# Splitting each expert's 64 slots into 32 per tile of tokens in a two-layer mixer and mixture-of-experts kernel

## The reference, cut to what matters

```
for l in range(2):
    x = layer_norm(alpha * x + mixers(x @ w_in[l]) @ w_out[l])
    score = sigmoid(x @ router_w)                  # 256 x 16
    best group of 4 experts, best 2 experts in it  # per token
    gate = the 2 scores, divided by their sum
    for e in range(16):
        h = silu(x @ w_gate[l][e]) * (x @ w_up[l][e])     # 1024 -> 512, twice
        out += gate[:, e:e+1] * (h @ w_down[l][e])        # 512 -> 1024
    x = layer_norm(alpha * x + out)
```

## Time and profile before

| | |
|---|---|
| time, median of 3 runs | 875.36 us (875.27 to 876.86) |
| span of the profiled execution | 876.5 us, mean granted TensorE clock 0.975 |
| TensorE busy | 832.4 us (95%) |
| DVE, ACT, POOL busy | 320.5, 182.2, 25.9 us |
| moved by DMA | 245.83 MB |
| experts' part, layer 0 and layer 1 | about 204 to 430 and 637 to 863 us |

### The profile page before, as it was taken

The page is one execution under the profiler, slowest core; times in us unless marked ns, Lnnn a source line. Parts: engine busy times, 40 slices in busy tenths (PEclk is TensorE's granted clock), DMA queues, the critical chain, the costliest instruction groups (busy, mean ns, idle before and its releaser), DMA issues. The chain is left out here.

```text
span 876.5 us, 12763 instructions
## 1 busy us (share of the span) xinstructions
PE 832.4 (95%) x5339; PEld 459.3 (52%) x5339; DVE 320.5 (37%) x644; ACT 182.2 (21%) x371; POOL 25.9 (3%) x101
## 2 busy tenths in 40 slices
PE   9999999989999999999799998999799999999994
PEld 8888666456334333333388876754543343333331
DVE  1296446474112111111434955292732211111215
ACT  1142323233001120000313233241330011100001
POOL 7100000000000000000000000000000000000000
PEclk9999999989999999999889999999899999999997
DMA  8944200496999999999944522025959999899992
GB/s 277 314 163 167 97 3 15 160 424 223 352 422 421 422 391 368 422 420 422 396 145 150 192 98 98 2 97 209 402 201 362 423 422 421 337 424 421 421 421 94
DMA packets 55249, 245.83 MB, mean 280 GB/s; under 512 B 8356, under 2 KB 13328, under 8 KB 30608
## 3 DMA queue, kind: packets, MB, share of 16 engines
q1 hardware_dynamic: 53840, 240.20, 69.3%
q0 software_dynamic: 1344, 4.72, 1.6%
HBM read 243.85 MB, written 1.05 MB: 279 GB/s over the span
## 5 line engine op out<-in xcount | busy, mean ns | idle before, releaser
L1047 PE MATMUL bank<-x_cm,ring 128*128 128x256 f32 x576 | 127.7, 383 | 0.9 <-ACT x_cm L2015 0.9
L549 PE MATMUL bank<-ring,xg 128*64 128x512 f32 x544 | 123.6, 596 | 2.0 <-issue 2.0
L1047 PEld LDWEIGHTS bank<-x_cm,ring 128*128 128x128 f32 x576 | 110.3, 192 | 17.3 <-ACT x_cm L2015 1.2
L780 DVE TENSOR_TENSOR y_lo<-bank,y_hi 128x512 fp32r<-128x512 f32 x32 | 22.1, 692 | 200.1 <-issue 179.8
L549 PE MATMUL bank<-ring_more,xg 128*64 128x512 f32 x416 | 94.6, 596 | 0.2 <-DMA ring_more<-in_exp_w_up 0.2
L549 PEld LDWEIGHTS bank<-ring,xg 128*64 128x64 f32 x544 | 37.5, 137 | 71.1 <-issue 69.4
L583 PE MATMUL bank<-ring,x_cm 128*64 128x512 f32 x256 | 61.2, 623 | 1.0 <-DVE g_col L756 1.0
L583 PE MATMUL bank<-ring_more,x_cm 128*64 128x512 f32 x256 | 58.2, 596 | 2.0 <-issue 2.0
L765 DVE TENSOR_SCALAR x_cm<-bank,g_col 128x512 f32<-128x512 f32 x32 | 24.0, 751 | 94.4 <-PE bank L549 79.7
L1054 PE MATMUL bank<-ring,x_cm 128*128 128x512 f32 x128 | 57.7, 599 | 0.0
L549 PEld LDWEIGHTS bank<-ring_more,xg 128*64 128x64 f32 x416 | 29.8, 137 | 52.9 <-issue 51.5
(11 more groups left out here) (387 smaller groups left out, 928.3 us busy)
## 6 DMA issues: line engine op xcount, KB each, us to landing
ring<-in_exp_w_gate SPq DMA_DIRECT2D x36, 1024.0 KB, 12.3
ring<-in_exp_w_up SPq DMA_DIRECT2D x36, 1024.0 KB, 12.9
ring_more<-in_exp_w_down SPq DMA_DIRECT2D x32, 1024.0 KB, 12.9
ring<-in_exp_w_down SPq DMA_DIRECT2D x32, 1024.0 KB, 11.8
ring_more<-in_exp_w_gate SPq DMA_DIRECT2D x26, 1024.0 KB, 12.5
ring_more<-in_exp_w_up SPq DMA_DIRECT2D x26, 1024.0 KB, 14.7
ring<-in_w_in SPq DMA_DIRECT2D x24, 1024.0 KB, 8.1
ring<-in_w_out SPq DMA_DIRECT2D x8, 1024.0 KB, 6.2
```

What stands on the lines that cost most here:

```text
L549: m = T.matmul(b[half_of(n, i), :], xg[g][:, 4 * h + k, cols], w[:, k, :], start=(h == 0 and k == 0), stop=(h == 1 and k == 3))
L780: mark(V.tensor_tensor(y_lo[:], y_bank(n, N)[:], y_hi[:].bitcast(F32), ALU.subtract), "v_ylo")
L1047: m = T.matmul(out_, w[:, k, c:c + n], x_cm[:, k, :], start=(k == 0), stop=(k == KD - 1))
```

## The change

An expert's 64 slots are no longer shared by both tiles: 32 (`HS`) belong to tile 0 and 32 to tile 1, and the running numbers start anew in each tile, with 128 added in tile 1. A branch flag is raised when an expert has more than 32 tokens in one tile.

- `pick[:, j]` has 256 columns instead of 512, and a gather's products have 256 columns each and write their own half of the bank. ACT puts the columns in the order expert, tile, slot while it copies.
- The scatter is still 8 products, each with 32 rows instead of 64; the four products of one part of y lie in four different groups of 32 rows.
- `position_row` is four products of 32 output partitions by 128 columns instead of one of 128 by 256; `pick_t` is compared over 128 columns.
- `slot_gates` has 16 products with 32 weight columns each, writing 32 partitions, instead of 8 products with 128.
- The count of the slots takes two products instead of five, and the positions are made in two DVE instructions, each followed by its tile's `pick`.

```diff
-        pick = sb("pick", [P, TT, GU * SL], F32R)
+        pick = sb("pick", [P, TT, GU * HS], F32R)
-        pick_t = sb("pick_t", [P, S], F32R)
+        pick_t = sb("pick_t", [P, P], F32R)
-        CROWD = SL + 0.5
+        CROWD = HS + 0.5
...
-                    m = T.matmul(out_[:], x[:, j, k, :], pick[:, j, :],
-                                 start=(j == 0 and x is x_hi), stop=(j == TT - 1 and x is x_lo))
+                    m = T.matmul(out_[:, GU * HS * j:GU * HS * j + GU * HS], x[:, j, k, :], pick[:, j, :],
+                                 start=(x is x_hi), stop=(x is x_lo))
...
-                    for j in range(TT):
-                        w = gate[:, j, e:e + 2] if rounds == 1 else gate[:, j, e:e + 1].to_broadcast([P, 2])
-                        m = T.matmul(b_y[:, u:u + 2], pick[:, j, u * SL:u * SL + 2 * SL].bitcast(F32), w,
-                                     start=(j == 0), stop=(j == TT - 1))
+                    for i in range(2):
+                        for j in range(TT):
+                            w = gate[:, j, e:e + 2] if rounds == 1 else gate[:, j, e:e + 1].to_broadcast([P, 2])
+                            at_slot = SL * i + HS * j
+                            m = T.matmul(b_y[at_slot:at_slot + HS, u:u + 2],
+                                         pick[:, j, (u + i) * HS:(u + i) * HS + HS].bitcast(F32), w, start=True, stop=True)
...
-                            ps = slice(SL * hf, SL * hf + SL)
-                            m = T.matmul(bank[2 * j + hf][:], pick_t[ps, tile_(j)], y[ps, :], start=(n == 0 and y is y_hi),
+                            ps = slice(SL * hf + HS * j, SL * hf + HS * j + HS)
+                            m = T.matmul(bank[2 * j + hf][:], pick_t[ps, :], y[ps, :], start=(n == 0 and y is y_hi),
...
-                mark(T.matmul(b_hid[n % 2][:, 0:S], ident_b[0:NE, e:e + 1].to_broadcast([NE, P]), pos_t[:],
-                              start=True, stop=True), "t_prow")
+                for q in range(P // HS):
+                    m = T.matmul(b_hid[n % 2][HS * q:HS * q + HS, 0:P], ident_b[0:NE, e:e + 1].to_broadcast([NE, HS]),
+                                 pos_t[:, tile_(q % TT)], start=True, stop=True)
+                mark(m, "t_prow")
...
-            return A.activation(out_, in_, ACT.Identity, scale=ln_cm[:, l, 0, k:k + 1], bias=ln_cm[:, l, 1, k:k + 1])
+            return A.activation(out_.rearrange("p (u j s) -> p j u s", u=GU, j=TT),
+                                in_.rearrange("p (j u s) -> p j u s", u=GU, j=TT), ACT.Identity,
+                                scale=ln_cm[:, l, 0, k:k + 1], bias=ln_cm[:, l, 1, k:k + 1])
...
-                T.matmul(bank[5][:, 0:NE], tri_b[:], sel_b[:, 0], start=True, stop=True)
-                T.matmul(bank[5][:, NE:2 * NE], tri_b[:], sel_b[:, 1], start=True, stop=False)
-                T.matmul(bank[5][:, NE:2 * NE], ones_b[:], sel_b[:, 0], start=False, stop=True)
-                T.matmul(bank[5][:, 2 * NE:3 * NE], ones_b[:], sel_b[:, 0], start=True, stop=False)
-                inc(T.matmul(bank[5][:, 2 * NE:3 * NE], ones_b[:], sel_b[:, 1], start=False, stop=True), "t_slots")
+                chosen = sel_b[:].rearrange("p j e -> p (j e)")
+                T.matmul(bank[5][:, 0:TT * NE], tri_b[:], chosen, start=True, stop=True)
+                inc(T.matmul(bank[5][:, TT * NE:2 * TT * NE], ones_b[:], chosen, start=True, stop=True), "t_slots")
...
-                do(V.scalar_tensor_tensor(out=pos[:], in0=bank[5][:, 0:TT * NE].rearrange("p (j e) -> p j e", j=TT), scalar=1.0,
-                                          in1=rank, op0=ALU.add, op1=ALU.mult))
-                for j in range(TT):
+                for j in range(TT):
+                    do(V.scalar_tensor_tensor(out=pos[:, j], in0=bank[5][:, NE * j:NE * j + NE], scalar=1.0 + P * j,
+                                              in1=rank[:, j], op0=ALU.add, op1=ALU.mult))
                     inc(pick_slots(0, 1, (j,)), "v_first")
```

More of the change, by code:

```diff
@@ L54, in hybrid_trunk @@
     SL = 64
+    HS = SL // TT
     ROUNDS = S // SL
@@ L453, in pick_slots @@
                 m = V.tensor_tensor(pick[:, j, :].rearrange("p (e s) -> p e s", e=per),
-                                    slot_row[:, 0:SL * rounds].unsqueeze(1).to_broadcast([P, per, SL * rounds]),
-                                    pos[:, j, g * per:g * per + per].unsqueeze(2).to_broadcast([P, per, SL * rounds]),
+                                    slot_row[:, P * j:P * j + HS * rounds].unsqueeze(1).to_broadcast([P, per, HS * rounds]),
+                                    pos[:, j, g * per:g * per + per].unsqueeze(2).to_broadcast([P, per, HS * rounds]),
                                     ALU.is_equal)
@@ L787, in turned_pick @@
                     dve.wait_ge(*at("t_scat", n))
-                mark(V.tensor_scalar(pick_t[:], b_hid[n % 2][:, 0:S], slot_col[:, r:r + 1], None, ALU.is_equal), "v_pick_t")
+                mark(V.tensor_scalar(pick_t[:], b_hid[n % 2][:, 0:P], slot_col[:, r:r + 1], None, ALU.is_equal), "v_pick_t")
             picks(0)
@@ L951, in _ @@
             step(G.iota(slot_row[:], [[1, S]], base=1, channel_multiplier=0, allow_small_or_imprecise_dtypes=True))
-            for h in range(2):
-                step(G.iota(slot_col[SL * h:SL * h + SL, :], [[SL, ROUNDS]], base=1, channel_multiplier=1,
+            for q in range(P // HS):
+                step(G.iota(slot_col[HS * q:HS * q + HS, :], [[HS, ROUNDS]], base=1 + P * (q % TT), channel_multiplier=1,
                             allow_small_or_imprecise_dtypes=True))
@@ L1971, in _ @@
                 dve.wait_ge(*done("t_slots", l))
-                do(V.scalar_tensor_tensor(out=pos[:], in0=bank[5][:, 0:TT * NE].rearrange("p (j e) -> p j e", j=TT), scalar=1.0,
-                                          in1=rank, op0=ALU.add, op1=ALU.mult))
                 for j in range(TT):
+                    do(V.scalar_tensor_tensor(out=pos[:, j], in0=bank[5][:, NE * j:NE * j + NE], scalar=1.0 + P * j,
+                                              in1=rank[:, j], op0=ALU.add, op1=ALU.mult))
                     inc(pick_slots(0, 1, (j,)), "v_first")
-                do(V.tensor_reduce(rms_s[:, 0, 1:2], bank[5][:, 2 * NE:3 * NE], AX.X, ALU.max))
+                do(V.tensor_reduce(rms_s[:, 0, 1:2], bank[5][:, TT * NE:2 * TT * NE], AX.X, ALU.max))
                 inc(V.tensor_scalar(crowded[:], rms_s[:, 0, 1:2], CROWD, None, ALU.is_gt), "v_flag")
```

## The result

The changed kernel takes 864.1 us (median of 4 runs, 862.2 to 866.47) against 875.32 us for the kernel before (4 runs, 873.3 to 876.86): a ratio of 0.9876, with a 95% interval of 0.985 to 0.9903, or 9 to 13 us less. The forecast was 860.0 us in a range of 854.5 to 867.5, so the time lies in the range, on its slow side. The gain is 11 us where 15 were expected. The profiled execution is the 866.47 us one, with a span of 864.6 us; before it was 876.5, so the two profiles differ by 11.9 us, and what follows splits up this figure.

What follows compares the result with a forecast made beforehand. TensorE and the weight-load queue were taken to end together, the queue being late next. Its 6.8 us plus 0.8 behind `hidden(15, 1)` make 7.6 a layer, 15.2 in all: 861.3 on the profile, 860 against the median, range 854.5 to 867.5.

Steps and rivals of the forecast that it cites:

- a faster TensorE alone: Rival for the whole kernel: TensorE sets the end after all, 13.0 us a layer gained, 849 us; chance 0.03.
- second hole: Drop in load traffic mid-part, lacking 4.0 us in layer 0 and 4.4 in layer 1; forecast to close, counted 3.8.
- The release that closes the hole: `hidden(8, 0)` frees the slot for `gate8`: forecast 8.9 us earlier, where 7.0 (7.4 in layer 1) were needed.
- the start of a part: First experts of each layer: `first_half` starts 1.95 us earlier, `hidden(0, 1)` and the releases after it 3.0.
- first hole: Low load traffic at the start of the experts, lacking 9.0 us; loads there wait for TensorE's next step.
- The queue's gain: Weight loads of each layer: 3.0 us earlier from the start plus 3.8 from the middle, 6.8 in all.
- Gate products: `slot_gates`: 32 records at 0.068 us, 2.1 against 1.84 us, so a loss of 0.3 us per group.
- Half clock: Rival: 1.2 GHz spells ahead of `hidden(0, 1)` or behind `hidden(15, 1)`, 1.9 us each, 862 to 866 us; chance 0.13.
- Gathers: Gather products of 256 columns follow each other every 0.122 us; a gather of four saves 0.42 us.
- The rule of the Trainium skill that was kept as a rival: Rival, only the scatter gains: a gather product's load and stream don't overlap, 218 ns each, 867 us; chance 0.08.
- Scatter: Each expert's scatter: quads of 32-row products run side by side, 0.66 us instead of 1.13, saving 0.47.
- The tail: Behind `hidden(15, 1)` in each layer: two scatters and two position rows, 0.8 us saved.

Runs made afterwards that it cites:

- gather_twice: Changed kernel with every gather product issued twice, the first of each pair overwritten: 868.08 us, ratio 0.9893 to the kernel before.
- the second profile: Changed kernel measured again with no edit: 865.16 us, ratio 0.9874 to the kernel before; this profile's span is 862.2 us.
- The edit of one count: Changed kernel, but DVE gives a count right behind the gate values and the first group's gate products wait for that: 860.21 us, ratio 0.9807.
- turn_pad: Changed kernel with one overwritten 256-column product more ahead of the transposes of experts 0 to 13: 866.65 us, ratio 0.9892 to the kernel before.
- light_after: Changed kernel with half of the columns of all loads of experts 8 to 15 left out: 848.4 us, ratio 0.9691 to the kernel before.
- before: The kernel before the change, unedited: 875.32 us.
- light_before: The kernel before with half of the columns of all loads of experts 8 to 15 left out: 874.87 us, ratio 0.9977.
- order_before: The kernel before with down7 loaded ahead of gate8 and up8: 875.91 us, ratio 0.9995.

## Why the prediction was right, and where it was off

**The bound was read rightly.** TensorE and the queue ended together before; a faster TensorE alone would have given 849, and the measured 848.4 with light loads answers to that. The queue then set the end in layer 0, at a place and in a form that were forecast: waits for up weights in experts 12 to 15, the longest 2.43 us where 2.9 were computed, and a closed second hole in both layers. In layer 1 the same waits are there, but `hidden(15, 1)` itself came 0.6 us behind its weights. (That 422 GB/s is "never exceeded" is loosely said: slices in the earlier trace rows reach 424. It changes nothing.) The agreement of 848.4 with 849 is closer than it deserves, as the next points show: it is in part luck.

**The release that closes the hole came 9.1 us earlier in layer 0** (329.56 became 320.49), where 8.9 were computed, but the terms are others. Computed: 3.0 for the start, 3.3 for scatters, 3.4 for gathers, -0.8 for position rows and gate products. Measured: 0.75 at the start, 7 steps x 0.19 = 1.3, 8 gathers x 0.45 = 3.6, and 3.1 around expert 4's gate products, 8.8 in all. Errors of 2.3 us (the start) and 1.5 (scatters with position rows) on one side and of 3.4 (gate products) on the other cancelled; that is luck. With a start that is hardly earlier, 4.0 us would have been enough to close the hole, and `gather_twice` shows it: its release is 4.65 earlier (324.91), and no dip is left.

**The step that fell short: the start of a part, "`hidden(0, 1)` and the releases after it come 3.0 us earlier".** It named ACT's four copies as late next. In layer 0 it was DVE's queue, 2.54 us, and then the half clock, 1.6 us; the releases came 2.1 and 0.75 earlier, and the first hole did not shrink at all. In the second profile, without the spell, the later of the two releases came 3.4 earlier, so this part of the prediction holds in some executions and not in others. In layer 1, where DVE was late by only 0.29 us, the second of them is 4.0 earlier, more than the 3.0. The prediction had looked at what the gathers wait for and what reads them, but not at the wait ahead of the gate products (`v_pick`), whose count DVE gives behind work that nobody at this place needs. The edit of one count is worth 4 to 6 us, and with it the kernel is at the 860 that was forecast; since the edit was no part of the forecast and other terms were off too, that figure is a coincidence. The queue's gain, 6.8 us by the prediction, was 3.5 in layer 0 and 7.4 in layer 1: the 3.3 us that are missing in layer 0 are as much as the 15.2 of the forecast lack against the 11.9 of the profile.

**Gate products: "+0.3 per group" was mis-sized and had the wrong sign.** They cost 1.4 us less, and no half clock follows in expert 4, another 1.7. The price came from a row of products that stream 128 columns each; these stream two. With 128 weight columns such a record costs 115 ns, with 32 it costs 13. The Trainium skill has a rule on the load ("TensorE: Matmul & The Clock Gate", LDWEIGHTS (loading the stationary operand)): it takes as many nanoseconds as it has weight columns, divided by 1.2, whatever the rows. That is 107 ns for 128 columns, with which the 0.11 of the earlier trace rows agrees, and 27 ns for 32, an estimate by that page of 0.85 us for 32 records. The trace has 0.43, half of that: on the same side as the rule and further. Why it is half, no run shows.

**Half clock: it was a rival of 0.13 and in part it came true,** ahead of `hidden(0, 1)` as it said, in one of two profiles of the changed kernel. What it did not say is that the change also takes spells away: those in expert 4. Two more stand behind waits for weights, in both profiles: the one at 385.26 (2.43 us of wait) lies under the queue, as TensorE waits again at 400.16 and 410.11, and the one at 825.18 (2.42) takes some 0.6 us. That is less than the 1.9 of the rival, which had put its spells where nothing is left to hide them.

**Gathers: 0.12 us per product, as forecast,** 0.45 us per gather where 0.42 were. The rule of the Trainium skill that was kept as a rival ("TensorE: Matmul & The Clock Gate", Part 3, What overlaps and what doesn't), that a load overlaps running products only for other rows of the array, doesn't hold here: these products have all 128 rows, and their loads of 0.19 us start every 0.12 us, under each other and under the streams.

```profile
206.54 0.19 PEld L427 LDWEIGHTS bank<-pick,x_lo 128*128 128x128 f32 x1
206.66 0.19 PEld L427 LDWEIGHTS bank<-pick,x_hi 128*128 128x128 f32 x1
```

**Scatter: 0.67 us, forecast 0.66.** But its saving of 0.47 is not a step's saving. The step shrank from 12.47 to 12.28 us, 0.19: the turn needs DVE's scaling of the hidden values, which takes 0.75 us from the last hidden product on. Before, the scatter of 1.13 hid it; now TensorE waits 0.24. Position rows gave 0.05 instead of costing 0.06. "What is late next" was asked about the start of a part and not about the step. Here it costs next to nothing, since the queue sets the pace there (`turn_pad`). It would be up to 28 x 0.24 us if TensorE did, an estimate.

**The tail** gave 0.53 per layer up to the start of `scatter(15)`: 0.48 for `scatter(14)`, 0.05 for a position row. The 0.47 of `scatter(15)` itself isn't seen in what follows in layer 0, since the next layer's first products are 4.06 us earlier (431.55 against 435.61) and no more; at the end of the kernel it may be part of the last 0.6. Computed were 0.8.

**ACT's copy** was put at 0.78 to 0.87 us. It takes 0.69 (2.78 for four). The old figure was set by the pace of the gather products that it waited for.

## What to carry to other kernels

When two resources end together, compute each one's gain by itself and expect the smaller; a run in which one of them is made artificially light measures both. When a stretch of an engine's work shrinks, list every wait behind it together with the place in the other engine's queue where the count is given: a count that comes behind unneeded work is invisible until its cover is gone. And price a product by what it loads and streams, each from its own rows, not by the nearest product of another shape.

## What the hardware showed beyond that

- Products with 32 weight columns and 2 streamed ones, going to four groups of 32 output partitions in turn, pass at 13 ns each (32 records in 0.43 us) and 11 ns (64 in 0.71), where those with 128 weight columns need 115 (16 in 1.84). When repeats to the same group lie in between, it is more: 128 records in 2.6 us, 20 ns.
- TensorE's clock fell to the 1.2 GHz level behind standstills of 2.54 us (5.24 us for sixteen products), of 2.23 (`turn_pad`) and 2.08 us (`light_after`), but the length of a standstill doesn't decide it: in one and the same profile of the changed kernel it fell behind 2.43 us (385.26) and 2.42 (825.18) and stayed up behind 2.41 (810.27, 3.65 us for sixteen products). It also fell behind 1.84 us of gate products with a wait of 0.51 us in expert 4, in both layers of every profile that has these products (`before`, `light_before`, `order_before`); behind 0.43 and 0.71 us of them it didn't. Cutting a stretch of tiny products short gave more (1.7 us of clock) than its own length (1.4 us).
